# Two attention items instead of one in each place between projection passes, with the steps around them moved and four probability buffers

## The chip, the cores and the metric

The kernel runs on one core of one Trainium2 chip. The metric is the time of one execution on the device in microseconds (us); the times given are medians of runs. Engines: TensorE (PE in the profile, PEld for its weight loads), VectorE (DVE), ScalarE (ACT), GpSimd (POOL) and SyncE (SP, which here issues most DMAs).

## The reference

Two layers over x of 512 tokens by 1024 channels in float32. A layer normalizes x, projects it onto 9,292 columns and feeds three branches:

- A: 8 heads of sparse attention. An indexer scores the keys, the 128 best of each query are kept, and softmax runs over these.
- B: 8 heads of chunked attention with a learned bias by relative position.
- C: an mLSTM with 4 heads of 128 channels. Its q and k pass a causal convolution of 4 taps and a silu first.

```python
def hybrid_layer(x, ...):
    h = rms_norm(x, norm_g)
    proj = jnp.einsum('bsd,de->bse', h, w_in) + b_in
    ...
    y_a = indexer_sparse_attention(a_q, a_k, a_v, i_q, i_k, i_w)
    y_b = chunked_relpos_attention(b_q, b_k, b_v, rel_bias)
    y_c = mlstm_chunkwise(silu(conv(c_q)), silu(conv(c_k)), c_v, c_i, c_f + f_bias, c_o)
    y_c = head_layer_norm(y_c, c_norm_w)
    branches = jnp.stack([y_a * silu(a_z), y_b * silu(b_z), y_c * silu(c_z)], axis=2)
    y = jnp.einsum('bsnw,nwd->bsnd', branches, w_branch)
    merged = jnp.sum(sigmoid(gates) * y, axis=2)
    return x + jnp.einsum('bsd,de->bse', merged, w_out)
```

## The kernel before, in words

**The projection.** It is cut into 49 units of 128 columns. Weights and activations are split into a high and a low float32r part, and a unit is 24 passes, matmuls of 128x128 weights with 512 columns (`product`, L626): 16 with the high weights (`w_hi`), then 8 with the low ones (`w_lo`). ScalarE makes the high part of a unit's weights (`high_part`, L825) and GpSimd the low part (`split`, L588), in two slots by turns. Units add up in two banks, `acc`, by turns. When a unit is done, ScalarE reads it out (`read_sums`, L854) and makes the high part of the unit after next. Units 16 to 48 are bq (up to 12 before), bk, bv (17 to 20), cq and ck (21 to 28), cv (29 to 32), az, bz (33 to 40), co, cz. Behind the units come a loop that merges the branches and the output projection.

**The items.** Branch A has items 0 to 31, item n being head n % 8 of query block t = n // 8; branch B items 32 to 63 and branch C items 64 to 79, with head (n - 32) // 4 or (n - 64) // 4 and block t = n % 4. An item of block t works on (t + 1) * 128 keys, in steps:

- `scores`: TensorE makes the scores in one of two banks (L722, L728; for C L737 to L744), VectorE adds the mask or bias and takes the maximum into a buffer of `prob` (L1302), which frees the bank.
- `exp`: ScalarE's exponential in `prob` (L1014, for C L1027).
- `turn_p`: TensorE transposes it (L753) into one of two banks, ScalarE copies it out to `prob_t` (L1038). For C VectorE multiplies instead (L1312).
- `values`: TensorE multiplies it with the values (L766, L773); behind every fourth item (every second of C) VectorE divides by the sums (L1322 to L1335).

**The order.** `schedule` (L84) writes out one list of steps, and each engine runs its own part of it in that order. Steps between two `CUT`s are a group. `interleave` (L233) sets the groups of a unit at even distances between the 24 passes of the next unit, so that a group is a place where TensorE leaves the passes for small matmuls. `push(n)` (L90) makes one group: the scores of item n, the exponential of item n - 1, the transposes of n - 2 and the values of n - 3 (for C all but the scores one item later: exponential of n, transposes of n - 1, values of n - 2). Units 17 to 37 have three or four such groups each, units 38 to 41 four and one for the z unit. Behind a group's attention steps stand, in the same place of each queue: a round of `topk` on VectorE (L1266, L1267); the stacks, that is the high and low parts of q and k of a head (`bq_hi`, `bk_hi` on ScalarE, L982 to L992; `bq_lo`, `bk_lo` on VectorE, L1250 to L1261), at the items of `STACK_AT` (L75 to L81); `rel_bias`, a DMA that ScalarE issues (L1004); and the steps below.

**Steps in the middle of a unit.** `conv` (L1271) runs on VectorE, for units 21 to 28, in two parts of two taps each; `conv_gate` is a tanh on ScalarE (L995) and a product on VectorE (L1287) that waits for it. Part 0 stands behind the last group of a unit, part 1 behind the first group of the next (`soon`), the gate behind its second (`late`). `turn_v` (TensorE and ScalarE), `y_split` (ScalarE L1042, then VectorE L1350) are in `late` too. `rows` (L1353 to L1372, with an Exp and an Ln on ScalarE, L1045 and L1047) stand one per unit behind item 31 on. `z_a`, `z_b` (L777, L1337) have groups of their own in units 34 to 41: TensorE transposes the branch's output into the bank `spare`, VectorE multiplies it with the read-out unit, and ScalarE's read-out of the next such unit waits for that (L863). `turn_c` (L785, L1373) uses `spare` as well.

```python
    for u in range(first, U_BZ):
        units(u, u + 1)
        upto = -(-64 * (u + 1 - first) // (U_BZ - first))
        k = 0
        while n < upto:
            push(n)
            if work:
                seq.append(work.pop(0))
            seq.extend(STACK_AT.get(n, []))
```

Of the kernel before, what the change touches and what calls it, by code (L numbers as in the profile page):

```python
# [26 lines left out]
P = 128  # L27
DEPTH, SEQ, D = 2, 512, 1024
NT = SEQ // P
DC = D // P  # L30
HEADS, HD = 8, 64
IDX_HEADS = 4
TOPK = 128
# [45 lines left out]
for h in range(1, HEADS):  # L79
    for n, kind in ((28, "bq_hi"), (29, "bk_hi"), (29, "bq_lo"), (30, "bk_lo")):  # L80
        STACK_AT.setdefault(n + 4 * h, []).append((kind, h))  # L81


def schedule(l):  # L84
# [5 lines left out]
    def push(n):  # L90


        seq.append(CUT)
        if n is not None:
            seq.append(("scores", n))
        flying.append(n)
        mlstm = any(m is not None and m >= 64 for m in flying[-4:])
        for back, kind in ((1, "exp"), (2, "turn_p"), (3, "values")) if mlstm else ((2, "exp"), (3, "turn_p"), (4, "values")):
            if len(flying) >= back and flying[-back] is not None:
                seq.append((kind, flying[-back]))  # L100

    def flush():
        for _ in range(3):
            push(None)
        flying.clear()
# [56 lines left out]
    for u in range(first, U_BZ):  # L162

        units(u, u + 1)
        upto = -(-64 * (u + 1 - first) // (U_BZ - first))
        k = 0
        while n < upto:
            push(n)
            if work:
                seq.append(work.pop(0))  # L170
            seq.extend(STACK_AT.get(n, []))
            if n == 31:
                rows = 0
            if n >= 32 and n % NT == NT - 1 and (n - 32) // NT + 2 < HEADS:
                seq.append(("rel_bias", (n - 32) // NT + 2))
            n += 1
            if k == 0:
                seq.extend(soon)
                soon = []
            if k == 1:  # L180
                seq.extend(late)
                late = []
                if rows == 6:
                    seq.append(("row_parts", 0))
                    rows += 1
                if u == U_AZ + 1:
                    seq.append(("turn_c", 0))
            k += 1
# [15 lines left out]
    for u in range(U_BZ, U_CO):  # L204
        units(u, u + 1)
        for k in range(NT):
            push(n)
            n += 1
            if k == 2:
                seq.extend(late)  # L210
                late = []
# [114 lines left out]
def build(nc, x_in, x_tok_in, w_full, w_mix, params_in, rel_in, gains_in, consts_in, out, x_kept):  # L326
    ctx = ExitStack()
    with ctx:
# [80 lines left out]
        ones = sb("ones", [P, SEQ])  # L409
# [7 lines left out]
        prob = sb("prob", [P, 3, SEQ])  # L417
# [202 lines left out]
        def _(pe):  # L620
# [57 lines left out]
            for l in range(DEPTH):  # L678
                for kind, n in SEQUENCES[l]:
# [67 lines left out]
                    elif kind == "turn_p":  # L747
                        branch, h, t = item(n)
                        if branch != "c":
                            pe.wait_ge(turn_free[n % 2], l * (ITEMS // 2) + n // 2 + FREE)  # L750
                            pe.wait_ge(prob_ready, l * ITEMS + n + 1)
                            for s in range(t + 1):
                                last = pe.transpose(ps_t[n % 2][:, s * P:(s + 1) * P], prob[:, n % 3, s * P:(s + 1) * P], ident)  # L753
# [65 lines left out]
        def _(act):  # L819
# [24 lines left out]
            for l in range(DEPTH):  # L844
# [65 lines left out]
                for kind, n in SEQUENCES[l]:  # L910
# [99 lines left out]
                    elif kind == "exp":  # L1010
                        branch, h, t = item(n)
                        if branch != "c":
                            act.wait_ge(max_ready, l * 64 + n + 1)
                            act.activation(prob[:, n % 3, 0:(t + 1) * P], prob[:, n % 3, 0:(t + 1) * P], ACT.Exp,  # L1014
                                           bias=neg_max[:, n % 4:n % 4 + 1], scale=-1.0,
                                           accum_out=row_sum[:, n % 8:n % 8 + 1]).then_inc(prob_ready, 1)
                        else:
                            use = SCORE_USE[("scores", n)]
                            act.wait_ge(score_full, l * SCORE_USES + use + 1)
                            if n < 67:  # L1020
                                act.wait_ge(turn_full, l * ITEMS + n - 2)
                            else:
                                act.wait_ge(turn_free[(n - 3) % 2], l * (ITEMS // 2) + (n - 3) // 2 + 1 + FREE)
                            if n == 64:
                                act.wait_ge(spare_free, l * SPARE_USES + SPARE_USE[("turn_c", 0)] + 3 + FREE)
                            for s in range(t + 1):
                                last = act.activation(prob[:, n % 3, s * P:(s + 1) * P], ps_s[use % 2][:, s * P:(s + 1) * P],  # L1027
# [76 lines left out]
        def _(dve):  # L1104
# [52 lines left out]
            for l in range(DEPTH):  # L1157
# [10 lines left out]
                for kind, n in SEQUENCES[l]:  # L1168
# [120 lines left out]
                    elif kind == "scores":  # L1289
# [3 lines left out]
                        if branch != "c":  # L1293
# [8 lines left out]
                            dve.tensor_tensor_reduce(out=prob[:, n % 3, 0:w], in0=ps_s[use % 2][:, 0:w], in1=mask, scale=-1.0,  # L1302
                                                     scalar=3.0e38, op0=ALU.add, op1=ALU.min,
                                                     accum_out=neg_max[:, n % 4:n % 4 + 1]).then_inc(max_ready, 1)
                    elif kind == "turn_p":
                        branch, h, t = item(n)
                        if branch == "c":
# [4 lines left out]
                            dve.scalar_tensor_tensor(prob_t[:, n % 2, 0:w], ps_t[n % 2][:, 0:w], 0.25 * P ** -0.5, prob[:, n % 3, 0:w],  # L1312
# [47 lines left out]
                    elif kind == "rows":  # L1360
# [3 lines left out]
                        link(dve.tensor_tensor_scan(decay[:, SUM_AT[s]:SUM_AT[s] + w], ones[0:CH, 0:w], f_row[:, s * P:SEQ], 0.0,  # L1364
# [175 lines left out]
```

## Time and profile before

| what | us |
|---|---|
| median of 3 runs (1302.51 to 1303.42) | 1303.11 |
| the profiled execution's own time | 1301.93 |
| its span, from the first instruction to the last | 1300.1 |
| TensorE busy | 1268.2 |
| VectorE busy | 697.6 |
| ScalarE busy | 618.4 |
| GpSimd busy | 601.6 |

The span is what the trace covers; 1.8 us of the execution lie outside it. Matmuls overlap in their records, and a record runs on for some time after the next has started, so what a matmul costs is read from one start to the next. The first layer's items lie between 113 and 363 us of the span, the second layer's between 750 and 1000 us, in the same pattern.

### The profile page before, as it was taken

What the parts mean: (1) busy time and instruction counts of PE and PEld (TensorE: products, weight loads), DVE (VectorE), ACT (ScalarE), POOL (GpSimd) and SP (SyncE); (2) the same over time, 40 slices, a digit from 0 to 9 for tenths busy, and PEclk for the clock granted to TensorE, in tenths of its full rate; (3) what the DMA queues carried; (4) which work ended last, traced back from release to release, by engine and by line L of the source; (5) the groups of instructions that cost most, each with busy time, mean ns of one, the idle gap of its engine ahead of it and who ended that gap; (6) DMA issues with size and microseconds to landing.
All of it is one profiled execution on the core that took longest, in us unless ns stands there. A gap on an engine that the chain in (4) does not pass through costs nothing.

```text
span 1300.1 us, 19666 instructions
## 1 busy us (share of the span) xinstructions
PE 1268.2 (98%) x6462; PEld 1063.8 (82%) x6462; DVE 697.6 (54%) x1422; ACT 618.4 (48%) x1119; POOL 601.6 (46%) x759
## 2 busy tenths in 40 slices
PE   8999999999999999999999999999999999999997
PEld 6787888888987888887878888888888878888875
DVE  6789797854445221123687888886544631121143
ACT  6444667675534332333244466677654433323332
POOL 6654333422235555455675633343322455455462
PEclk9999999999999999999999999999999999999998
DMA  7223111221322323323242221112112222332331
GB/s 276 97 83 110 68 50 57 69 86 49 112 68 61 108 82 97 107 87 120 87 160 83 96 87 60 50 65 90 58 49 103 85 81 83 103 99 86 105 97 65
DMA packets 37047, 116.35 MB, mean 89 GB/s; under 512 B 4080, under 2 KB 4464, under 8 KB 36720
## 3 DMA queue, kind: packets, MB, share of 16 engines
q1 hardware_dynamic: 34672, 111.24, 25.8%
q10 hardware_dynamic: 2304, 4.20, 1.1%
q8 instruction: 41, 0.67, 0.2%
q14 instruction: 30, 0.25, 0.1%
HBM read 111.23 MB, written 4.19 MB: 89 GB/s over the span
## 4 chain that ended last, share of the span: by engine, by line
PE 82%; DVE 10%; ACT 4%; issue 3%; POOL 1%; DMA 0%; ACTq 0%; SPq 0%; DVEq 0%; POOLq 0%
PE acc L639 66%; PE ps_o L766 4%; PE ps_t L753 3%; DVE score L1267 2%; PE ps_t L744 2%; PE ps_o L773 1%; PE ps_s L722 1%; DVE top L1266 1%; PE ps_s L728 1%; DVE att_c L1399 1%; DVE ak_s L1240 1%; PE spare L704 1%; ACT prob L1014 1%; PE ps_s L737 1%; PE spare L783 1%
## 5 line engine op out<-in xcount | busy, mean ns | idle before, releaser
L593 POOL TENSOR_TENSOR w_lo<-w_raw,w_hi 128x256 fp32r<-128x256 f32 x744 | 588.6, 820 | 674.9 <-ACT w_hi L831 674.6
L639 PE MATMUL acc<-h_hi,w_hi 128*128 128x512 f32 x1120 | 448.1, 400 | 1.6 <-POOL h_lo L604 1.6
L639 PE MATMUL acc<-h_lo,w_hi 128*128 128x512 f32 x1120 | 439.2, 392 | 0.0
L639 PE MATMUL acc<-h_hi,w_lo 128*128 128x512 f32 x1120 | 293.0, 395 | 1.3 <-POOL w_lo L593 1.3
L831 ACT ACTIVATE w_hi<-w_raw 128x1024 fp32r<-128x1024 f32 (+1 forms) x210 | 201.9, 961 | 120.8 <-PE acc L639 92.0
L639 PEld LDWEIGHTS acc<-h_hi,w_hi 128*128 128x128 f32 x1120 | 210.8, 188 | 41.9 <-POOL h_lo L604 2.5
L639 PEld LDWEIGHTS acc<-h_lo,w_hi 128*128 128x128 f32 x1120 | 210.8, 188 | 39.0
L639 PEld LDWEIGHTS acc<-h_hi,w_lo 128*128 128x128 f32 x1120 | 205.3, 188 | 41.5 <-POOL w_lo L593 1.8
L1412 DVE SCALAR_TENSOR_TENSOR gated<-prob,acc 128x512 f32<-128x512 f32 x16 | 11.0, 687 | 247.6 <-PE acc L639 247.6
L1064 ACT ACTIVATE prob<-acc,par_half 128x512 f32<-128x512 f32 x48 | 33.1, 690 | 148.1 <-PE acc L639 148.1
L1014 ACT ACTIVATE prob<-prob,neg_max 128x128 f32<-128x128 f32 (+3 forms) x128 | 70.6, 552 | 19.7 <-DVE neg_max L1302 19.2
L1038 ACT ACTIVATE prob_t<-ps_t 128x128 f32<-128x128 f32 (+3 forms) x128 | 54.3, 425 | 34.2 <-PE ps_t L753 34.2
L753 PE MATMUL ps_t<-consts,prob 128*128 128x128 f32 x320 | 56.6, 275 | 7.1 <-ACT prob L1014 6.8
L1266 DVE MAX8 top<-score 128x8 f32<-128x256 f32 (+2 forms) x96 | 53.6, 558 | 1.6
L1302 DVE CUSTOM_DVE_ANT_0 prob<-ps_s,rel 128x128 f32<-128x128 f32 (+1 forms) x64 | 31.2, 490 | 40.6 <-PE ps_s L728 39.8
L1267 DVE MATCH_REPLACE8 score<-top,score 128x256 f32<-128x256 f32 (+2 forms) x96 | 52.1, 543 | 0.0
L639 PE MATMUL acc<-merged_hi,w_hi 128*128 128x512 f32 x128 | 50.8, 397 | 1.1 <-DVE merged_lo L1421 1.1
L753 PEld LDWEIGHTS ps_t<-consts,prob 128*128 128x128 f32 x320 | 38.9, 140 | 15.3 <-issue 10.4
L639 PE MATMUL acc<-merged_lo,w_hi 128*128 128x512 f32 x128 | 50.6, 395 | 0.0
L1412 DVE SCALAR_TENSOR_TENSOR z<-prob,acc 128x512 f32<-128x512 f32 x32 | 22.0, 687 | 50.8 <-PE acc L639 50.8
L1281 DVE SCALAR_TENSOR_TENSOR turn<-pad,par,turn 128x512 f32<-128x512 f32 x48 | 46.1, 961 | 1.5
L766 PE MATMUL ps_o<-av,prob_t 128*128 128x64 f32 x320 | 43.0, 265 | 1.3 <-issue 1.3
(242 smaller groups left out, 1787.9 us busy)
## 6 DMA issues: line engine op xcount, KB each, us to landing
w_raw<-w_full SPq DMA_DIRECT2D x162, 512.0 KB, 3.4
w_raw<-w_mix SPq DMA_DIRECT2D x48, 256.0 KB, 2.6
rel<-rel ACTq DMA_DIRECT2D x16, 256.0 KB, 2.6
xT<-x SPq DMA_DIRECT2D x4, 512.0 KB, 6.4
stage<-x_tok SPq DMA_DIRECT2D x4, 512.0 KB, 10.2
xT<-x SPq DMA_DIRECT2D x1, 2048.0 KB, 10.8
x_kept<-xT SPq DMA_DIRECT2D x1, 2048.0 KB, 9.0
xT<-x_kept SPq DMA_DIRECT2D x1, 2048.0 KB, 8.3
```

What stands on the lines that cost most here:

```text
L593: last = pool.tensor_tensor(w_lo[:, slot, part, :], w_raw[:, raw, part, :], w_hi[:, slot, part, :].bitcast(F32), ALU.subtract)
L639: last = pe.matmul(acc[slot][:, :], w[:, slot, k, :], x[:, k, :], start=(i == 0), stop=(i == 3 * nk - 1))
L753: last = pe.transpose(ps_t[n % 2][:, s * P:(s + 1) * P], prob[:, n % 3, s * P:(s + 1) * P], ident)
L766: last = pe.matmul(ps_o[:, place * HD:(place + 1) * HD], prob_t[:, n % 2, s * P:(s + 1) * P], v[:, s, f:f + HD], start=(s == 0), stop=(s = ...
L831: act.activation(w_hi[:, slot, 0:nk, :], w_raw[:, raw, 0:nk, :], ACT.Copy).then_inc(w_hi_done, 1)
L1014: act.activation(prob[:, n % 3, 0:(t + 1) * P], prob[:, n % 3, 0:(t + 1) * P], ACT.Exp, bias=neg_max[:, n % 4:n % 4 + 1], scale=-1.0, accu ...
L1038: act.activation(prob_t[:, n % 2, 0:(t + 1) * P], ps_t[n % 2][:, 0:(t + 1) * P], ACT.Copy)\
L1064: act.activation(prob[:, b, :], acc[slot_of(l, PROJ + b)][:, :], ACT.Tanh, bias=par_half[:, bass.ds(i * 2 + (C_GATE + DC * b + j), 1)], sc ...
L1266: link(dve.max(top8[:, :], s))
L1267: link(dve.match_replace(s, top8[:, :], s, TAKEN))
L1281: ins = dve.scalar_tensor_tensor(turn[:, :], x[:, tap:tap + SEQ], w, turn[:, :], ALU.mult, ALU.add)
L1412: dve.scalar_tensor_tensor((gated, z, z)[b][:, :], prob[:, b, :], 1.0, acc[slot_of(l, PROJ + 3 + b)][:, :], ALU.add, ALU.mult)\
```

## The change

- An attention place holds two items, n and n + 1: both scores, both exponentials, the transposes of the two before, the values of the two before these. With items of C in flight the transposes (VectorE's product) are those of the same two items, and the values those of the two before. `push(None)` of the three flushes becomes one or two empty places.
- The items of a unit, 3 or 4 before, are 2 or 4, so that units have one or two such places.
- All steps of `soon` and `late` stand behind the first place of a unit: part 1 of a convolution and its gate in one place.
- Stacks of B: `bq_hi` and `bk_hi` of head h behind item 27 + 4h, `bq_lo` and `bk_lo` behind item 29 + 4h.
- `prob` has four buffers instead of three; the array `ones` has 128 columns instead of 512, and the scan of `rows` reads one column of it as a broadcast.

```diff
+PROBS = 4
...
-    for n, kind in ((28, "bq_hi"), (29, "bk_hi"), (29, "bq_lo"), (30, "bk_lo")):
+    for n, kind in ((27, "bq_hi"), (27, "bk_hi"), (29, "bq_lo"), (29, "bk_lo")):
         STACK_AT.setdefault(n + 4 * h, []).append((kind, h))
...
-    def push(n):
+    def push(*items):
         seq.append(CUT)
-        if n is not None:
-            seq.append(("scores", n))
-        flying.append(n)
-        mlstm = any(m is not None and m >= 64 for m in flying[-4:])
-        for back, kind in ((1, "exp"), (2, "turn_p"), (3, "values")) if mlstm else ((2, "exp"), (3, "turn_p"), (4, "values")):
-            if len(flying) >= back and flying[-back] is not None:
-                seq.append((kind, flying[-back]))
+        seq.extend(("scores", n) for n in items)
+        flying.append(items)
+        seq.extend(("exp", n) for n in items)
+        lag = 0 if any(n >= 64 for new in flying[-2:] for n in new) else 1
+        for back, kind in ((lag, "turn_p"), (lag + 1, "values")):
+            if len(flying) > back:
+                seq.extend((kind, n) for n in flying[-1 - back])

     def flush():
-        for _ in range(3):
-            push(None)
+        push()
+        if not any(n >= 64 for new in flying for n in new):
+            push()
         flying.clear()
...
-        upto = -(-64 * (u + 1 - first) // (U_BZ - first))
+        upto = 2 * -(-32 * (u + 1 - first) // (U_BZ - first))
         k = 0
         while n < upto:
-            push(n)
-            if work:
-                seq.append(work.pop(0))
-            seq.extend(STACK_AT.get(n, []))
-            if n == 31:
-                rows = 0
-            if n >= 32 and n % NT == NT - 1 and (n - 32) // NT + 2 < HEADS:
-                seq.append(("rel_bias", (n - 32) // NT + 2))
+            push(n, n + 1)
+            for n in (n, n + 1):
+                if work:
+                    seq.append(work.pop(0))
+                seq.extend(STACK_AT.get(n, []))
+                if n == 31:
+                    rows = 0
+                if n >= 32 and n % NT == NT - 1 and (n - 32) // NT + 2 < HEADS:
+                    seq.append(("rel_bias", (n - 32) // NT + 2))
             n += 1
             if k == 0:
-                seq.extend(soon)
-                soon = []
-            if k == 1:
-                seq.extend(late)
-                late = []
+                seq.extend(soon + late)
+                soon, late = [], []
...
-        for k in range(NT):
-            push(n)
-            n += 1
+        for k in range(0, NT, 2):
+            push(n, n + 1)
+            n += 2
...
-        ones = sb("ones", [P, SEQ])
+        ones = sb("ones", [P, P])
...
-        prob = sb("prob", [P, 3, SEQ])
+        prob = sb("prob", [P, PROBS, SEQ])
...
-                            if n < 67:
-                                act.wait_ge(turn_full, l * ITEMS + n - 2)
+                            if n < 64 + PROBS:
+                                act.wait_ge(turn_full, l * ITEMS + n - PROBS + 1)
                             else:
-                                act.wait_ge(turn_free[(n - 3) % 2], l * (ITEMS // 2) + (n - 3) // 2 + 1 + FREE)
+                                act.wait_ge(turn_free[(n - PROBS) % 2], l * (ITEMS // 2) + (n - PROBS) // 2 + 1 + FREE)
...
-                        link(dve.tensor_tensor_scan(decay[:, SUM_AT[s]:SUM_AT[s] + w], ones[0:CH, 0:w], f_row[:, s * P:SEQ], 0.0,
+                        link(dve.tensor_tensor_scan(decay[:, SUM_AT[s]:SUM_AT[s] + w], ones[0:CH, 0:1].broadcast_to([CH, w]), f_row[:, s * P:SEQ], 0.0,
```

## Rows read from the trace of the kernel before

**Rows 1.** The page, part 1: busy time, share of the span, instructions.

```profile
PE 1268.2 (98%) x6462; PEld 1063.8 (82%) x6462; DVE 697.6 (54%) x1422; ACT 618.4 (48%) x1119; POOL 601.6 (46%) x759
```

**Rows 2.** Chain that ended last: start us, us, what.

```profile
406.62 196.60 PE acc L639 x864
```

**Rows 3.** Timeline of TensorE, two places: start us, us, instruction.

```profile
371.14 0.60 PE L798 MATMUL spare<-consts,z_tanh 128*128 128x128 f32 x4
...
371.81 0.40 PE L639 MATMUL acc<-h_lo,w_hi 128*128 128x512 f32 x1
...
204.99 0.61 PE L722 MATMUL ps_s<-ak_s,aq_s 128*128 128x512 f32 x2
205.45 0.60 PE L753 MATMUL ps_t<-consts,prob 128*128 128x128 f32 x4
205.88 1.00 PE L766 MATMUL ps_o<-av,prob_t 128*128 128x64 f32 x8
...
207.01 0.39 PE L639 MATMUL acc<-h_lo,w_hi 128*128 128x512 f32 x1
```

**Rows 4.** Windows: PE, PEld, DVE, ACT, POOL busy (count), clock, DMA share, GB/s.

```profile
116.00:130.00 14.00, 12.79 (x67) 10.55 (x66) 13.33 (x43) 7.95 (x24) 5.78 (x7) 1.00 0.22 70
170.00:222.00 52.00, 49.70 (x295) 42.92 (x295) 43.06 (x85) 35.82 (x70) 18.61 (x20) 1.00 0.14 46
222.00:280.00 58.00, 57.74 (x350) 50.49 (x349) 40.61 (x89) 42.93 (x94) 23.31 (x25) 1.00 0.26 87
280.00:314.00 34.00, 32.58 (x202) 27.80 (x201) 18.53 (x40) 20.59 (x46) 9.31 (x12) 1.00 0.18 55
314.00:363.00 49.00, 48.84 (x336) 43.77 (x336) 22.92 (x61) 23.47 (x56) 11.18 (x16) 1.00 0.26 86
```

**Rows 5.** Timeline of ScalarE and then TensorE around 213 to 221 us.

```profile
213.88 0.63 ACT L1045 ACTIVATE norm<-norm 4x512 f32<-4x512 f32 x1
214.53 1.28 ACT L1047 ACT_TABLE_LOAD   x1
...
218.37 1.28 ACT L1014 ACT_TABLE_LOAD   x1
...
218.37 0.39 PE L728 MATMUL ps_s<-bk_lo_s,bq_s 128*128 128x512 f32 x1
220.41 0.41 PE L753 MATMUL ps_t<-consts,prob 128*128 128x128 f32 x2 [1.65 <-ACT prob L1014]
```

**Rows 6.** VectorE's waits, 154 to 250 us: us in total, times, longest.

```profile
DVE prob L1302 <- PE ps_s L722: 6.1, 6, 1.9
DVE ck L1287 <- ACT z_tanh L995: 3.2, 2, 2.1
DVE prob L1302 <- PE ps_s L728: 2.7, 3, 1.3
```

**Rows 7.** Groups of VectorE, 116 to 363 us: busy us, mean ns | idle before.

```profile
L1281 DVE SCALAR_TENSOR_TENSOR turn<-pad,par,turn 128x512 f32<-128x512 f32 x24 | 23.1, 961 | 0.7
...
L1266 DVE MAX8 top<-score 128x8 f32<-128x512 f32 x16 | 11.0, 688 | 0.0
L1267 DVE MATCH_REPLACE8 score<-top,score 128x512 f32<-128x512 f32 x16 | 10.8, 675 | 0.0
...
L1302 DVE CUSTOM_DVE_ANT_0 prob<-ps_s,rel 128x512 f32<-128x512 f32 x8 | 5.5, 690 | 1.2 <-PE ps_s L728 1.1
...
L1278 DVE TENSOR_SCALAR turn<-pad,par 128x512 f32<-128x512 f32 x8 | 4.3, 544 | 0.2
...
L1287 DVE SCALAR_TENSOR_TENSOR ck<-z_tanh,turn 128x512 f32<-128x512 f32 x4 | 2.8, 692 | 3.2 <-ACT z_tanh L995 3.2
```

**Rows 8.** The same groups of ScalarE.

```profile
L831 ACT ACTIVATE w_hi<-w_raw 128x1024 fp32r<-128x1024 f32 x24 | 25.4, 1060 | 4.7 <-ACT pad L906 2.8 <-ACT z L867 2.0
...
L1014 ACT ACTIVATE prob<-prob,neg_max 128x512 f32<-128x512 f32 x16 | 11.4, 712 | 3.8 <-DVE neg_max L1302 3.8
...
L995 ACT ACTIVATE z_tanh<-turn 128x512 f32<-128x512 f32 x8 | 5.1, 633 | 7.3 <-DVE turn L1281 6.3 <-DVE neg_max L1302 0.9
```

More of the change, by code:

```diff
@@ L752, in _ @@
                             for s in range(t + 1):
-                                last = pe.transpose(ps_t[n % 2][:, s * P:(s + 1) * P], prob[:, n % 3, s * P:(s + 1) * P], ident)
+                                last = pe.transpose(ps_t[n % 2][:, s * P:(s + 1) * P], prob[:, n % PROBS, s * P:(s + 1) * P], ident)
                             last.then_inc(turn_full, 1)
@@ L1013, in _ @@
                             act.wait_ge(max_ready, l * 64 + n + 1)
-                            act.activation(prob[:, n % 3, 0:(t + 1) * P], prob[:, n % 3, 0:(t + 1) * P], ACT.Exp,
+                            act.activation(prob[:, n % PROBS, 0:(t + 1) * P], prob[:, n % PROBS, 0:(t + 1) * P], ACT.Exp,
                                            bias=neg_max[:, n % 4:n % 4 + 1], scale=-1.0,
@@ L1026, in _ @@
                             for s in range(t + 1):
-                                last = act.activation(prob[:, n % 3, s * P:(s + 1) * P], ps_s[use % 2][:, s * P:(s + 1) * P],
+                                last = act.activation(prob[:, n % PROBS, s * P:(s + 1) * P], ps_s[use % 2][:, s * P:(s + 1) * P],
                                                       ACT.Exp, bias=source_t[:, s, h:h + 1])
@@ L1300, in _ @@
                                 mask = key_mask[:, MASK_AT[t]:MASK_AT[t] + w] if t else consts[:, K_CHUNK:K_CHUNK + P]
-                            dve.tensor_tensor_reduce(out=prob[:, n % 3, 0:w], in0=ps_s[use % 2][:, 0:w], in1=mask, scale=-1.0,
+                            dve.tensor_tensor_reduce(out=prob[:, n % PROBS, 0:w], in0=ps_s[use % 2][:, 0:w], in1=mask, scale=-1.0,
                                                      scalar=3.0e38, op0=ALU.add, op1=ALU.min,
@@ L1311, in _ @@
                             w = (t + 1) * P
-                            dve.scalar_tensor_tensor(prob_t[:, n % 2, 0:w], ps_t[n % 2][:, 0:w], 0.25 * P ** -0.5, prob[:, n % 3, 0:w],
+                            dve.scalar_tensor_tensor(prob_t[:, n % 2, 0:w], ps_t[n % 2][:, 0:w], 0.25 * P ** -0.5, prob[:, n % PROBS, 0:w],
                                                      ALU.mult, ALU.mult).then_inc(turn_free[n % 2], 1)
```

## The prediction

> **What bounds the kernel now.** I read the page first. TensorE is busy for 98% of the span [rows 1], and its granted clock is 1.00 in every stage shown [rows 4], so the question is what stands between its matmuls. The chain of waits answers it for the back of a layer: 864 passes in 196.60 us, 0.2275 us each, with nothing between them [rows 2]. The change leaves that part alone. It touches units 16 to 41 of each layer, about 113 to 363 us and 750 to 1000 us, where attention's small matmuls stand in "places" between the passes of the projection.
>
> What does a place cost? The timeline of TensorE shows one place with 4 small matmuls and one with 2 wide and 12 small [rows 3]. The first takes 371.81 - 371.14 = 0.67 us up to the second pass behind it; less that one pass, 0.44, or 0.111 each. The second takes 207.01 - 204.99 - 0.227 = 1.79; less two 512-column matmuls (0.455), 1.34 for 12, again 0.111 each. A place thus has a price per matmul and none of its own.
>
> So only waits can be won or lost. By stage [rows 4] TensorE idles 2.30 us in 170 to 222, 0.26 in 222 to 280, 1.42 in 280 to 314 and 0.16 in 314 to 363. Records run over the start of a wait: the wait in [rows 5] is 1.65 in its row, but 220.41 - 218.37 less a pass is 1.8. With 0.15 more for each of some ten waits these stages hold about 3.5, 2.1 and 0.3 us (170 to 280, 280 to 314, 314 to 363); 1.6 more lie at the first items (116 to 130: 1.21 idle and three such overlaps) [rows 4]. That is 7.5 us a layer, 15 us in all: the most that the change can win.
>
> VectorE is the engine behind it: busy 43.06 of 52 us and 40.61 of 58 [rows 4]. Between 154 and 250 us it waits 8.8 us for scores and 3.2 for the tanh of the convolution [rows 6].
>
> **The change, part by part.**
>
> Places: 85 attention places a layer become 43, with the same matmuls. By [rows 3] this saves 42 x 0 = 0 on TensorE. The fit of those two places leaves about 0.03 us a place open either way, so the bounds are -1.3 and +1.3 us a layer; I take 0, the value both rows give.
>
> Four probability buffers, the smaller array of ones, its broadcast in the scan: the same count of instructions on VectorE; a shorter fill on GpSimd, hidden behind the load of x at the start. 0; without that cover it would be some tenths of a us, once.
>
> Stacks of branch B, and the bias DMAs on ScalarE's queue: same instructions and DMAs, at other items. Their users stand two places later as before. 0 by themselves; they count below as work in the queues.
>
> Convolution (units 21 to 28, eight a layer). Here I see the cost. Before, part 1 of a convolution stands in one place and its gate in the next, so ScalarE's tanh runs while VectorE does something else; only two of the eight gates wait, 3.2 us [rows 6]. After, both sets of steps go behind the same first place: VectorE finishes part 1 and stands at the gate until ScalarE has run the tanh (0.63, [rows 8]) and both handoffs (0.15): at least 0.8 x 8 = 6.4 us. Queued behind the waiting gate are the next part 0 and the next two masks; for those wait ScalarE's exponentials, and TensorE for both. ScalarE itself runs the tanh only after two exponentials, two copies and the stack copies of that place.
>
> How much of it reaches TensorE? I laid the three queues beside each other from the scores of items 16 and 17 (0 us, the trace's 155), with [rows 7] and [rows 8]: a topk round 0.69 + 0.68 and a short load between, 1.46, a mask of 512 columns 0.69, part 0 of a convolution 0.54 + 0.96 = 1.5, part 1 1.94, gate 0.7, an exponential 0.71, the high part of a unit 1.06. Waits of TensorE that come out:
> - at 22.9 (scores 24, 25): VectorE comes from gate 0 and part 0 of the next at 22.4, so masks 22, 23 end at 22.9 and 23.4; the copies of items 20, 21 stand behind those exponentials and free the transposes' banks at 24.7 and 25.2. Wait 1.1.
> - at 31.4 (scores 26, 27): the same with gate 1, done at 30.8. Wait 1.25.
> - ScalarE then is late: masks 30, 31 at 50.6, their exponentials and two copies to 52.6, stacks to 54.5, Exp, table load and Ln to 57.15, unit 26 read out and unit 28's high part to 59.0 (TensorE wants it at 59.65), table load, exponentials 32, 33 and copies to 62.35, tanh to 62.95. VectorE has stood at gate 4 since 58.85. It runs gate, rows and part 0 until 67.2 before masks 34, 35, and TensorE is there at 66.3: wait 2.1.
> - the debt stays: masks 40, 41 wait for part 0 of the last convolution until 89.1, TensorE is there at 85.8: wait 3.7.
> - small ones at 45.7, 96.8 and 101.6: 0.8.
>
> Sum 9.0 a layer, against about 3.5 in the same stretch now: **+5.5**. Bounds: +8.9 (all of the eight gates' added idle, 12.1 by this laying less the 3.2 of now, in TensorE's way) and -3.5 (all present waits gone and no new one). I take +5.5, as laid: VectorE has little reserve there, 8.8 us of waits for scores [rows 6], and what lies of it ahead of the convolutions can't take up what the gates add.
>
> The wait of now behind the table load goes: load, exponential, transpose in line [rows 5]. After, 20 passes (4.5 us) stand between the scores of items 32, 33 and their transposes. Late next is the gate named above; this is in the 9.0.
>
> A load takes 1.28 us and starts 0.02 us after the Exp before it [rows 5]. The Trainium skill, "ScalarE: Activation LUTs", What ACT_TABLE_LOAD costs, adds a drain of about 1.38 us to every switch; the trace shows none. By that page ScalarE would reach unit 28's high part 0.7 us too late for TensorE, and the sum would be some 1.5 us higher over both layers.
>
> Units 34 to 37: the transposes there wait because ScalarE reads out the z unit late, behind VectorE's gated product (1.42 idle, [rows 4]). With pairs there is a whole place and 6 passes or more behind the exponentials; only one wait, of z_a1 for the spare bank behind turn_c, comes out (0.4). 2.1 becomes 0.5: **-1.6**. Bounds -2.1 and 0.
>
> mLSTM items: values one place after their scores, 6 passes (1.36 us) and the next pair's scores between; the read-out of a unit holds ScalarE about 2.5 us. By the same laying it fits with 0.1 to spare in units 38 to 40 and misses by 0.5 in unit 41, where 4 and 5 passes stand; the present 0.3 at the last item goes. **+0.2**; bounds -0.3 and +2. First items: the masks still wait for the same topk rounds, 0.
>
> Sum a layer: 0 + 5.5 - 1.6 + 0.2 = +4.1; a hand laying tends to add up small lags that real slack takes away, and I take 3.7. Two layers: +7.4. Against the profiled execution (1301.93 us, span 1300.1) that is 1309.3; the median of the runs is 1.2 higher (1303.11), so **1310.5**.
>
> **The rivals.**
> A. Pairs give slack and nothing is given back (faster). For it: the wait behind the table load (1.8) and the z stage (1.7) and the last mLSTM item (0.3) each have their mechanism removed; if ScalarE is free at each gate, a gate costs 0.8 and VectorE's waits for scores take that up. It decides at whether the masks of items 34 to 41 are done when TensorE comes for the banks: if VectorE's debt stays below about 3 us there, nothing is lost. Then -3.8 a layer: 1303.1 - 7.6 = 1295.5. Against it: VectorE busy 43 of 52 us.
> B. Waits change places only: the new ones equal the lost 3.8 a layer. 1303.
> C. The debt also reaches the read-out: where a unit has one place, ScalarE reads out a finished unit only behind the tanh, and the high part of the unit after next comes late. My laying leaves 0.65 us at unit 28; 1 us less at each of four such units and TensorE stops at their start: +4 a layer more, 1318.
> D. The place has a price of its own that two rows don't show; bounds above, inside A and B.
>
> **How the numbers follow.** Forecast case (1306 to 1315) 0.44, C (to 1320) 0.08, B (1300.5 to 1305.7) 0.16, A (1290 to 1300.4) 0.32. About 0.2%, 2.6 us, is what a measurement of this kernel can tell. Slower 0.52, same 0.16, faster 0.32. The range leaves out half of A's lower side and what exceeds C: 1295 to 1319; the forecast's own range is 1306 to 1315.
>
> **What would show it.** Right: VectorE's wait for z_tanh rises from 3.2 to about 12 us a layer, TensorE's idle in the second half of the convolutions' stretch from 0.26 to 4 or more, all behind VectorE's masks; the transposes' wait behind the table load and in units 34 to 37 is gone. A pass stays 0.227. Wrong: if the gates wait near 0.8 each and the masks of items 34 to 41 are never waited for, A holds; if the time falls though the waits stay, places did have a price.

## The result, and the profile after

| | before | after |
|---|---|---|
| median of 4 runs each (us) | 1302.88 | 1316.59 |
| lowest to highest | 1302.51 to 1303.42 | 1314.73 to 1317.74 |
| ratio, with its 95% interval | | 1.0105 [1.0093, 1.0118] |
| the profiled execution | 1301.93 | 1317.74 |
| its span | 1300.1 | 1316.0 |

The change costs 13.7 us. It is slower, as forecast. The time lies inside the stated 1295 to 1319, but 1.6 us above the forecast case's own 1306 to 1315; the forecast was +7.4.

The page's part 1 and its clock line (40 slices, the granted clock in tenths), of after:

```profile
PE 1279.5 (97%) x6462; PEld 1073.1 (82%) x6462; DVE 699.0 (53%) x1422; ACT 613.9 (47%) x1119; POOL 595.7 (45%) x759
PEclk9999999999999999999999999988999999999998
```

Counts are those of [rows 1]: no instruction was added. New are the two slices at 8 ahead of the end, some 855 to 920 us; the 8 in the last slice stands in before too. The chain of waits gives the loss by layer; its rows of 864 passes start 7.76 us later than [rows 2] in the first layer, and in the second, where the chain of before has its row at 1044.04, 15.86 later. Of the first 7.76 us, 1.6 are lost near 35 us, ahead of all that was changed, in a spell at half clock (last section). So the items of the first layer lose 6.2 us and those of the second 8.1:

```profile
414.38 196.59 PE acc L639 x864
...
1059.90 196.60 PE acc L639 x864
```

Windows of after, columns as in [rows 4], where the last two rows cut out the place of the loss:

```profile
116.00:130.00 14.00, 13.34 (x72) 11.02 (x71) 13.37 (x43) 8.12 (x22) 6.04 (x8) 1.00 0.17 59
170.00:222.00 52.00, 50.91 (x299) 43.36 (x297) 41.16 (x81) 34.39 (x67) 15.76 (x19) 1.00 0.15 52
222.00:280.00 58.00, 53.39 (x294) 45.97 (x295) 39.22 (x85) 39.38 (x88) 18.88 (x23) 0.94 0.23 77
280.00:314.00 34.00, 32.35 (x204) 28.29 (x203) 21.06 (x44) 21.23 (x48) 10.86 (x12) 1.00 0.18 56
314.00:363.00 49.00, 49.00 (x338) 44.16 (x338) 20.91 (x56) 24.79 (x60) 13.45 (x20) 1.00 0.26 87
222.00:262.00 40.00, 35.39 (x184) 30.07 (x185) 32.95 (x66) 24.73 (x57) 13.28 (x15) 0.91 0.18 60
864.00:904.00 40.00, 36.36 (x175) 30.48 (x174) 31.15 (x63) 23.71 (x55) 13.56 (x16) 0.83 0.19 60
```

TensorE idles 4.61 us in 222 to 280, where it was 0.26, and here its mean clock is 0.94. Elsewhere little is left or gained: it idles 1.09 in 170 to 222 for 2.30 before, 0 for 0.16 in 314 to 363, and 1.65 for 1.42 in 280 to 314. Waits of VectorE (154 to 256 us, the same masks as 154 to 250 in before), then of TensorE (116 to 370 us): us in total, times, longest.

```profile
DVE ck L1287 <- ACT z_tanh L995: 8.4, 4, 4.1
DVE cq L1287 <- ACT z_tanh L995: 2.8, 4, 0.7
DVE prob L1302 <- PE ps_s L728: 2.6, 2, 1.4
DVE prob L1302 <- PE ps_s L722: 2.2, 2, 1.9
```

```profile
PE ps_s L728 <- DVE neg_max L1302: 4.1, 3, 2.5
PE spare L783 <- DVEq L1377: 1.6, 1, 1.6
PE ps_t L753 <- ACT prob_t L1038: 1.6, 3, 0.6
PE ps_s L722 <- DVE neg_max L1302: 0.6, 1, 0.6
```

All eight gates now wait for the tanh, 11.2 us against 3.2 [rows 6], and the waits of VectorE for scores fell from 8.8 to 4.8: of its reserve about half is used up. TensorE's waits for exponentials ([rows 5] shows the longest) are gone; in before this was their line:

```profile
PE ps_t L753 <- ACT prob L1014: 3.3, 5, 1.7
```

In their place TensorE waits 4.7 us for VectorE's masks, which it did once and for 1.0 us in before, and 1.6 each for `spare` and for ScalarE's copies of transposes.

The longest gate wait and the mask behind it, timeline of VectorE, then ScalarE in the same us, then TensorE:

```profile
212.51 1.54 DVE L1281 SCALAR_TENSOR_TENSOR turn<-pad,par,turn 128x512 f32<-128x512 f32 x2
218.16 0.69 DVE L1287 SCALAR_TENSOR_TENSOR ck<-z_tanh,turn 128x512 f32<-128x512 f32 x1 [4.11 <-ACT z_tanh L995]
218.89 0.68 DVE L1358 SCALAR_TENSOR_TENSOR f_row<-f_row,norm 4x512 f32<-4x512 f32 x1
219.60 1.21 DVE L1359 TENSOR_TENSOR_SCAN run_max<-f_row,i_iw_row 4x512 f32<-4x512 f32 x1
220.85 0.79 DVE L1278 TENSOR_SCALAR turn<-pad,par 128x512 f32<-128x512 f32 x1
221.68 1.10 DVE L1281 SCALAR_TENSOR_TENSOR turn<-pad,par,turn 128x512 f32<-128x512 f32 x1
222.82 0.56 DVE L1302 CUSTOM_DVE_ANT_0 prob<-ps_s,rel 128x384 f32<-128x384 f32 x1
```

```profile
213.28 1.06 ACT L831 ACTIVATE w_hi<-w_raw 128x1024 fp32r<-128x1024 f32 x1 [0.17 <-ACT pad L906]
214.36 1.28 ACT L1014 ACT_TABLE_LOAD   x1
215.66 0.40 ACT L1014 ACTIVATE prob<-prob,neg_max 128x128 f32<-128x128 f32 x1
...
216.55 1.06 ACT L1038 ACTIVATE prob_t<-ps_t 128x512 f32<-128x512 f32 x2
217.50 0.63 ACT L995 ACTIVATE z_tanh<-turn 128x512 f32<-128x512 f32 x1
```

```profile
221.57 0.39 PE L639 MATMUL acc<-h_lo,w_hi 128*128 128x512 f32 x1
223.44 0.33 PE L728 MATMUL ps_s<-bk_hi_s,bq_s 128*128 128x128 f32 x1 [1.48 <-DVE neg_max L1302]
```

VectorE has ended part 1 at 214.05 and stands until 218.16. ScalarE is at that time behind its own list: weights, a table load, the exponentials and copies of the place, and only then the tanh. Behind the gate stand the rows and part 0 of the next convolution, so the masks of items 34 and 35 start at 222.82, and TensorE, ready at 221.80 (221.57 and a pass), starts at 223.44: 1.64 us. This is gate 4, and the wait is that of the forecast's third station. ("Station" is used here for each of the four large waits of TensorE in the forecast's list: 22.9, 31.4, 66.3 and 85.8 us behind 155, so 177.9, 186.4, 221.3 and 240.8.)

**How each stretch is read.** Here and below "excess" is the time from each start on TensorE to the next, less 0.228 per 512 columns (0.173 for 384) and at least 0.111 per small matmul, near the prices of [rows 2] and [rows 3]; it is what waits and slow passes cost, free of overlaps in records. A price of 0.227 would add 0.3 to each entry of the long stretch, in all kernels alike. Of each kernel one profiled execution, first layer / second layer:

| excess, us | before | after | gate behind part 1 in before (b_gate_next) | gate a place later (a_gate_later) | unread matmuls in waits (a_fill_all) |
|---|---|---|---|---|---|
| 116–130 / 753–768 | 1.66 / 1.60 | 1.41 / 1.21 | 1.65 / 1.67 | 1.39 / 0.34 | 1.37 / 1.24 |
| 170–280 / 808–917 | 3.6 / 3.7 | 10.9 / 13.2 | 9.5 / 8.5 | 0.6 / 0.4 | 4.2 / 4.2, and 5.9 of them |
| 280–314 / 917–951 | 2.15 / 2.43 | 1.71 / 1.71 | 2.59 / 2.19 | 1.81 / 1.97 | 1.84 / 1.79 |
| 314–363 / 951–1000 | 0.24 / 0.22 | -0.22 / -0.18 | -0.21 / 0.47 | -0.27 / -0.19 | -0.32 / -0.24 |

The last column's 5.9 us are 26 unread matmuls of 0.227 a layer.

### The profile page after: what moved, and what is told of

Its sections match the earlier page's. It is cut to its first block, busy times and chain, and to the rows that moved or that the text cites. A ratio compares the mean times of both kernels' runs of the same rounds, so it can differ in the third digit from the quotient of the medians.

```text
span 1316.0 us, 19638 instructions
## 1 busy us (share of the span) xinstructions
PE 1279.5 (97%) x6462; PEld 1073.1 (82%) x6462; DVE 699.0 (53%) x1422; ACT 613.9 (47%) x1119; POOL 595.7 (45%) x759
## 4 chain that ended last, share of the span: by engine, by line
PE 74%; DVE 17%; ACT 5%; issue 2%; POOL 1%; DMA 0%; ACTq 0%; SPq 0%; DVEq 0%; POOLq 0%
PE acc L639 61%; PE ps_o L766 3%; DVE score L1267 2%; DVE top L1266 2%; DVE turn L1281 2%; PE ps_t L753 2%; PE ps_t L744 1%; PE ps_o L773 1%; DVE prob L1302 1%; PE ps_s L728 1%; DVE att_c L1399 1%; DVE bk_lo_s L1259 1%; PE ps_s L722 1%; DVE turn L1278 1%; ACT prob L1014 1%
## 5 line engine op out<-in xcount | busy, mean ns | idle before, releaser
L639 PEld LDWEIGHTS acc<-h_hi,w_lo 128*128 128x128 f32 x1120 | 211.3, 192 | 45.2 <-POOL w_lo L593 1.8
L753 PE MATMUL ps_t<-consts,prob 128*128 128x128 f32 x320 | 48.1, 280 | 3.8 <-ACT prob_t L1038 3.6
L1038 ACT ACTIVATE prob_t<-ps_t 128x128 f32<-128x128 f32 (+3 forms) x128 | 48.1, 419 | 6.1 <-PE ps_o L766 6.1
L766 PE MATMUL ps_o<-bv,prob_t 128*128 128x64 f32 x320 | 42.3, 283 | 0.0
L766 PEld LDWEIGHTS ps_o<-bv,prob_t 128*128 128x128 f32 x320 | 41.5, 205 | 0.2
```

The costliest lines, as they stand in the source:

```text
L639: last = pe.matmul(acc[slot][:, :], w[:, slot, k, :], x[:, k, :], start=(i == 0), stop=(i == 3 * nk - 1))
L766: last = pe.matmul(ps_o[:, place * HD:(place + 1) * HD], prob_t[:, n % 2, s * P:(s + 1) * P], v[:, s, f:f + HD], start=(s == 0), stop=(s = ...
L1038: act.activation(prob_t[:, n % 2, 0:(t + 1) * P], ps_t[n % 2][:, 0:(t + 1) * P], ACT.Copy)\
```

## The experiments

Twelve kernels; each ratio is to the kernel before on the same chip, with its 95% interval. Names beginning with b_ are edits of the kernel before, with a_ of the one after; "pairs" are the two items in one place. The expectations put two theories against each other: by theory 1 the loss is the gate's wait for the tanh, by theory 2 it is the coarser order of the pairs.

**b_gate_next: only the gate moves, in the kernel before.** One item per place and everything else stays.

```diff
-            late.append(("conv_gate", u - U_CQ))
+            soon.append(("conv_gate", u - U_CQ))
```

> The kernel before, with one item per place as it is, and only the gate of a convolution moved up behind part 1, in the first place of a unit. If the gate behind part 1 is what costs (theory 1), VectorE's waits for z_tanh rise from 3.2 us a layer to 6 or more and part of that reaches TensorE: 2 to 8 us slower than before. If the loss needs the pairs, because two masks and two exponentials stand behind each other and the banks are wanted one place earlier (theory 2), this kernel stays within 2 us of the kernel before, though its gates wait.

Measured 1315.13 us against 1302.19, 1.0100 [1.0083, 1.0117], +12.9: this one word gives nearly the whole loss. The waits of VectorE, and those of TensorE (same stretches as above):

```profile
DVE ck L1287 <- ACT z_tanh L995: 2.8, 4, 0.7
DVE cq L1287 <- ACT z_tanh L995: 2.8, 4, 0.7
```

```profile
PE ps_t L753 <- ACT prob L1014: 6.0, 8, 1.7
PE ps_o L766 <- issue: 1.3, 1, 1.3
```

Every gate waits exactly 0.7, the round trip for the tanh. VectorE waits for the tanh only 2.4 us longer than before, and yet TensorE loses 5 to 6 us a layer. The gate and its wait, 1.4 us, now stand ahead of the next mask, and the delay comes out at the transposes: TensorE's waits there for exponentials are 6.0 us in eight places, for 3.3 in five. That it comes out there because with one item per place the transposes follow their scores soon is argued, not shown. So the place of the gate is dear in both kernels, but by another wait than in the kernel after. The loss is above the 2 to 8 us of theory 1 and the 2 of theory 2; a spell at half clock (last section) is part of it.

**a_no_tanh and b_no_tanh: the wait taken away in both.** The tanh of the silu is left out and the gate reads `turn` alone.

```diff
-                        act.wait_ge(conv_sum, l * 8 + n + 1)
-                        act.activation(z_tanh[:, :], turn[:, :], ACT.Tanh, scale=0.5).then_inc(conv_tanh, 1)
+                        continue
...
-                        dve.wait_ge(conv_tanh, l * 8 + n + 1)
+                        dve.wait_ge(conv_sum, l * 8 + n + 1)
...
-                        dve.scalar_tensor_tensor(dst, z_tanh[:, :], 1.0, turn[:, :], ALU.add, ALU.mult).then_inc(conv_done, 1)
+                        dve.scalar_tensor_tensor(dst, turn[:, :], 1.0, turn[:, :], ALU.add, ALU.mult).then_inc(conv_done, 1)
```

> The changed kernel without the tanh of the convolution's gate, so nothing of ScalarE's is waited for at the gate; VectorE's two instructions stay. It leaves the tanh out of silu. Theory 1: the gates' wait (11.2 us a layer) was the loss, so the waits of TensorE for masks at 221 and 243 us go and the time falls by 9 us or more, to 1307 or below, with the granted clock at 1.00 in the items. Theory 2: VectorE's debt comes from the coarser order, and the time falls by less than 4 us.

> The kernel before, with the same tanh left out: the control. Its gates wait 3.2 us a layer now and ScalarE gets 5 us of work less; both theories expect 0 to 3 us less than before, 1300 to 1303.

Measured: after 1295.52, 0.9944 [0.9928, 0.9961]; before 1301.75, 0.9995 [0.9986, 1.0005]. Leaving the tanh out is worth nothing that shows in before (0.4 us) and 21 us in after, as theory 1 had it. Without it the kernel with pairs is 6.2 us faster than the one without. In a_no_tanh TensorE is busy nearly without a gap in the stretch that idled 4.61:

```profile
170.00:222.00 52.00, 51.85 (x315) 45.30 (x314) 46.79 (x89) 34.77 (x71) 19.01 (x20) 1.00 0.19 61
222.00:280.00 58.00, 57.29 (x341) 49.63 (x340) 40.34 (x90) 41.99 (x94) 20.15 (x24) 1.00 0.25 79
```

**a_conv_first: other work between part 1 and the gate, in the same place.** Part 1 and the tanh go right behind the attention steps; topk rounds and stacks stand between them and VectorE's gate.

```diff
             push(n, n + 1)
+            if k == 0:
+                seq.extend(soon)
+                seq.extend(("conv_tanh", step[1]) for step in late if step[0] == "conv_gate")
+                soon = []
```

> The changed kernel with the same steps, pairs kept: in the first place of a unit, part 1 of the convolution and ScalarE's tanh stand right behind the attention steps, and the topk rounds and stacks stand between them and VectorE's gate. Theory 1: the gates' wait falls from 11.2 us a layer to under 3 and the time by 6 us or more. Theory 2: less than 3 us.

Measured 1302.18, 0.9999 [0.9990, 1.0009]: the time of before, 14.4 us under after. The time is as theory 1 had it; the gates' wait, expected under 3 us, is 4.6. Four waits of 0.7 (cq) are gone and 4.6 of 8.4 (ck) is left, the longest 3.2, at gate 4 as in after.

**a_gate_later: the gate one place later, the tanh left behind part 1.** The sums of two convolutions are then alive at once, so they alternate between `turn` and `gated`.

```diff
             push(n, n + 1)
+            seq.extend(gates)
+            gates = []
...
-                seq.extend(soon + late)
+                seq.extend(soon)
+                gates = [step for step in late if step[0] == "conv_gate"]
+                seq.extend(("conv_tanh", step[1]) for step in gates)
+                seq.extend(step for step in late if step[0] != "conv_gate")
...
+                        total = (turn, gated)[n % 2]
```

> The changed kernel with whole computation: ScalarE's tanh right behind part 1 of a convolution, VectorE's gate one place later (even and odd convolutions sum up in two buffers, so that the next may start). Pairs kept. If the gates' waits were the only loss and the pairs themselves win what the two kernels without a tanh show (6.2 us), the gates wait near 0 and the time is 1295 to 1298, faster than before. If ScalarE's queue stays the bound, the gates still wait over 3 us a layer and the time is 1301 or more.

Measured 1293.61 against 1301.79, 0.9936 [0.9922, 0.9949]. No gate waits, and its windows show idle time of 0.15 us at most and no drop of the clock:

```profile
170.00:222.00 52.00, 52.00 (x316) 45.82 (x316) 47.63 (x94) 38.64 (x78) 20.24 (x21) 1.00 0.20 63
222.00:280.00 58.00, 57.85 (x345) 50.53 (x344) 41.59 (x87) 42.96 (x96) 21.06 (x24) 1.00 0.26 81
```

That is faster than the 1295 to 1298 expected. No instruction is left out against the kernel after, so the whole step from +13.7 to -8.2 is one of place. The 7.3 us of excess in the stretches of the convolutions of before (3.6 + 3.7) are down to 1.0: this is what the pairs are good for. That it is not only the wait at the gates shows in b_no_tanh, where these waits are gone too and the same stretches still have 3.5 and 3.4.

**a_gate_turnc: that, and turn_c right behind the attention steps.** It is aimed at z_a1's wait for `spare`.

```diff
+            if k == 0 and u == U_AZ + 1:
+                seq.append(("turn_c", 0))
...
-                if u == U_AZ + 1:
-                    seq.append(("turn_c", 0))
```

> The same, with turn_c right behind the attention steps of its place instead of behind the stacks and y_split, so that z_a1 finds the spare bank free. If TensorE's wait of 1.8 us at L783 around 290 us is VectorE's two copies standing behind those steps, it goes: 3 to 3.6 us less than a_gate_later over two layers. If it is passed on to the next wait (VectorE's gated product, ScalarE's read-out of the z unit), less than 1 us.

Measured 1291.36 against 1301.79, 0.9920 [0.9907, 0.9934]: 10.4 us under before, the best of all. The wait of 1.8 for `spare` is gone, but a part of it comes back in another place, timeline of TensorE:

```profile
292.64 0.28 PE L733 MATMUL ps_s<-bk_lo_s,bq_s 128*128 128x256 f32 x1
293.65 0.55 PE L758 MATMUL ps_t<-consts,prob 128*128 128x128 f32 x3 [0.73 <-ACT prob_t L1043]
```

The excess of 280 to 314 goes from 1.81 to 0.87, and 1.97 to 1.00 in the second layer: 1.9, for 2.25 measured. The gain lies between the two outcomes that the expectation names.

**b_ones_prob: four buffers, the small array of ones and its broadcast, in the kernel before.**

```diff
-        ones = sb("ones", [P, SEQ])
+        ones = sb("ones", [P, P])
...
-        prob = sb("prob", [P, 3, SEQ])
+        prob = sb("prob", [P, PROBS, SEQ])
...
```

> The kernel before with four probability buffers, the array of ones at 128 columns and the broadcast in the scan, nothing else. All theories expect no change: 1302 to 1304. Only if the earlier start of TensorE's first matmuls (ones are filled 0.4 us sooner) changes its clock at the head, 1.5 us more.

Measured 1302.09 against 1301.79, 1.0002 [0.9993, 1.0012]: nothing, as the forecast had it.

**a_stacks_old and a_later_stacks_old: the stacks at their old items**, in the kernel after and in a_gate_later.

```diff
-    for n, kind in ((27, "bq_hi"), (27, "bk_hi"), (29, "bq_lo"), (29, "bk_lo")):
+    for n, kind in ((28, "bq_hi"), (29, "bk_hi"), (29, "bq_lo"), (30, "bk_lo")):
```

> The changed kernel with branch B's stacks at the items of before (28, 29, 29, 30). Theory 1 (the gates): the stack copies stand on ScalarE ahead of the tanh in either case, at other gates; within 2 us of the changed kernel, 1314 to 1318. If the stacks' new items were what delayed ScalarE (its tanh 4.1 us late at the longest wait), 4 us or more faster.

> a_gate_later (gates one place later, pairs kept) with branch B's stacks at the items of before. With the gates right behind part 1 those items cost 7.7 us more. If that came through the gates and VectorE's debt, here it costs under 1.5 us: 1293 to 1295. If the low parts of k come too late for the first scores of a head in any case (the pair's first place is one place behind them), 4 us or more: 1298 or above.

Measured 1324.29, 1.0169 [1.0154, 1.0185], which is 7.7 over after; and 1310.76 against 1302.04, 1.0068 [1.0055, 1.0082], some 17 us above a_gate_later. The first of these was a clear miss of mine (1314 to 1318 expected); the second is as expected if the low parts come too late. Waits of VectorE and TensorE in a_later_stacks_old:

```profile
DVE bq_s L1258 <- ACT bq_s L992: 9.7, 4, 4.9
```

```profile
PE ps_s L733 <- DVE bk_lo_s L1264: 5.6, 3, 3.3
```

In pairs items 28 and 29 (32 and 33 for the first of these heads) share a place, so VectorE's `bq_lo` stands in the place of ScalarE's `bq_hi` and waits for it: the same fault as the gate's, at another step. `bk_lo` then comes in the last place ahead of the scores of its head. With 27 and 29 the high parts stand a place ahead, and neither wait is there. The moved stacks are not neutral: they are what the pairs need.

**a_rows_later: rows from item 33 on instead of 31**, to take their Exp, Ln and table loads out of ScalarE's way at gate 4.

> The changed kernel with the steps rows (Exp and Ln on ScalarE with their table load) one unit later, behind item 33 instead of 31. If gate 4's wait of 4.1 us comes from ScalarE's table loads standing ahead of its tanh, it falls to about 0.8 at this gate but one of the next two gates pays part of it; the time falls by 2 to 8 us. If it stands only behind masks and exponentials, it stays and the time is within 1 us of the changed kernel.

Measured 1317.13, 1.0117 [1.0100, 1.0133]: no gain. The waits of ck are 8.5 in total for 8.4, but they have moved. Timeline of VectorE, gates 4 and 5:

```profile
215.07 1.15 DVE L1287 SCALAR_TENSOR_TENSOR ck<-z_tanh,turn 128x512 f32<-128x512 f32 x1 [0.70 <-ACT z_tanh L995]
...
226.96 0.69 DVE L1287 SCALAR_TENSOR_TENSOR ck<-z_tanh,turn 128x512 f32<-128x512 f32 x1 [5.18 <-ACT z_tanh L995]
```

Gate 4 waits 0.70 for 4.11 in after, and gate 5, ahead of which Exp, Ln and the two table loads now stand, 5.18 for 1.66. So ScalarE's lag at gate 4 does come from these steps, and a place one unit later only hands it to the next gate; this half of the expectation came true, the gain of 2 to 8 us did not.

**a_fill and a_fill_all: is it the clock?** The granted clock fell in the kernel after (below). Unread matmuls of 512 columns into `spare` stand ahead of the scores of items 36 and 42, where TensorE would wait: 6 and 8 in a_fill, 7 and 19 in a_fill_all, whose edit this is.

```diff
+                        for _ in range({36: 7, 42: 19}.get(n, 0)):
+                            pe.matmul(spare[:, :], h_hi[:, 0, 0:P], h_hi[:, 0, :], start=True, stop=True)
```

> The changed kernel with 6 matmuls of 512 columns that nobody reads (1.36 us) just before the scores of item 36 and 8 (1.8 us) before those of item 42, in the two places where TensorE waits 1.6 and 2.7 us for a bank anyway. If its waits there are what is followed by spells at half the granted clock, these go, the clock is 1.00 from 220 to 260 and from 860 to 905 us, and the time falls by the 8 us that passes and small matmuls lose in them, to 1308 to 1310; if the spells have another cause, they stay and the time does not fall.

> The changed kernel with 7 and 19 unread matmuls (1.6 and 4.3 us) before the scores of items 36 and 42, since with 6 and 8 TensorE still waited 2.7 us at item 42 and one spell at half clock stayed. If a wait of TensorE is what goes ahead of a spell, none is left from 220 to 260 and 860 to 905 us. Then what the spells cost can be read: if they add to the waits, 1309 to 1312 (they hold 20 us at half clock); if VectorE sets the time of these places and the spells only fill its waits, within 2 us of the changed kernel.

a_fill: 1317.61 against 1301.85, 1.0119 [1.0102, 1.0135], no gain, where 1308 to 1310 was expected. The spells at 226 and 868 were gone; TensorE came earlier to item 42, still waited (2.3 for the mask), and the spell behind it at 247 was twice as long. a_fill_all: 1312.19 against 1302.04, 1.0076 [1.0063, 1.0090], with no spell left in either layer's items:

```profile
222.00:262.00 40.00, 38.85 (x220) 33.03 (x220) 32.20 (x67) 26.02 (x60) 12.94 (x16) 1.00 0.21 71
864.00:904.00 40.00, 38.84 (x217) 32.71 (x217) 32.53 (x68) 25.71 (x58) 12.96 (x16) 1.00 0.21 68
```

VectorE's waits for the tanh are as in after, 8.4 and 2.8. It is 10.15 us slower than before (1312.19 less 1302.04), where after is 13.7 slower, each against the kernel before measured beside it; that leaves 3.6 us for the clock, and the two medians taken as they stand 4.4 (1316.59 less 1312.19). So 3.6 to 4.4 of the 13.7 us go with the clock, and some 9.3 to 10.1 are the waits. Unread matmuls that outlast the waits they fill would raise the clock's share; this was not measured.

## Why the prediction was right or wrong

**The number.** The sign and the mechanism came true. The size did not: +13.7 for +7.4, and 1316.59 lies where the forecast had put the outcomes of rival C (up to 1320, chance 0.08) and not its own. That it is inside the range is owed to the room left for C, whose mechanism is not what happened; this part is luck. Of the 6.3 us missed, 2.7 are waits whose sum was too small (10.15 less 7.4, with a_fill_all for full clock), and the rest, 3.6, goes with the clock.

**Places 0: borne out, within the bounds.** With half of the places, a_gate_later has an excess of 0.6 and 0.4 in the convolutions' stretches, priced by matmuls alone; a place that cost much more than [rows 3] say would have made it negative. The -0.2 to -0.3 in 314 to 363 leave room for some tenths a layer. The bounds of 1.3 stand (rival D).

**Buffers, array of ones, broadcast 0: right**, by b_ones_prob.

**The gates: right in mechanism and nearly in size.** Forecast 12.1 us of gate waits a layer, measured 11.2 (+8.0 on before instead of +8.9). The four stations came in the order and within 3 us of the places laid by hand, 6.7 us in sum for 8.2:

| forecast at (us of trace) | wait forecast | measured at | measured |
|---|---|---|---|
| 177.9 | 1.1 | 179.8 | 0.67 |
| 186.4 | 1.25 | 188.0 | 0.71 |
| 221.3 | 2.1 | 221.6 | 1.64, 0.34, 0.68 in one place |
| 240.8 | 3.7 | 243.5 | 2.65 |

"What lies of it ahead of the convolutions can't take up what the gates add" held: VectorE's waits for scores fell by 4.0 us, not enough for 8.0. The step +5.5 a layer compares with 10.9 - 3.6 = 7.3 and 13.2 - 3.7 = 9.5, clock included. At full clock (a_fill_all) it is 4.2 + 5.9 - 3.6 = +6.5. Not all of that must be waits: the unread matmuls may be a few tenths longer than the waits they fill. The fourth station is larger at full clock than in the table: 2.65 us stand in the trace of after only since TensorE came to it late from a spell of 3.4 us; in a_fill_all 19 unread matmuls, 4.3 us, stand there for the 3.7 forecast.

**The clock: not in the forecast at all.** "A pass stays 0.227" is wrong behind four of TensorE's waits (last section). This is the largest miss, 3.6 to 4.4 of the 6.3 us between +7.4 and +13.7.

**Units 34 to 37: mis-sized.** The step was forecast at -1.6, from 2.1 to 0.5; the excess went from 2.15 to 1.71 and from 2.43 to 1.71, so -0.4 and -0.7. The number that failed is z_a1's wait for `spare` behind turn_c, named at 0.4. Timeline of TensorE, and of ScalarE:

```profile
296.64 0.39 PE L639 MATMUL acc<-h_lo,w_hi 128*128 128x512 f32 x1
298.68 0.66 PE L783 MATMUL spare<-consts,att_a 128*128 128x128 f32 x4 [1.65 <-DVEq L1377]
```

```profile
301.73 0.69 ACT L866 ACTIVATE z_tanh<-acc,par_half 128x512 f32<-128x512 f32 x1 [6.11 <-DVE gated L1345]
```

298.68 - 296.64 less a pass is 1.8. VectorE frees `spare` only behind the low stacks and y's low part of that place, and the forecast gave this 0.4 in all. ScalarE's wait of 6.11 holds no one up: behind 298.68 TensorE has no wait for 17 us.

**mLSTM items and first items: better than forecast.** 0.24 to -0.22 and 0.22 to -0.18, so -0.4 instead of +0.2; the miss by 0.5 at unit 41 did not come. The first items gave 0.25 and 0.4 where 0 was taken, though in that stretch of the second layer a_gate_later has 0.34, so its size differs between executions or kernels by more than that.

**The cut from 4.1 to 3.7** ("small lags that real slack takes away") took the wrong side: at full clock the sum is near 5.1 a layer (10.15 / 2) for 4.1 laid.

**Stacks "0 by themselves": the sum is right, the reason wrong.** It compared with their users, two places later as before. It did not ask where the high part that `bq_lo` waits for is made. Had the change left the stacks at their old items, the same argument would have given the same 0, and the time would have been 7.7 us longer.

**Rivals.** A, pairs win, has the right mechanism and was refused by the gates: take their wait away and 1293.6 to 1295.5 comes out, for 1295.5 forecast. Its deciding point, a debt of VectorE below about 3 us at items 34 to 41, was missed. C, the debt reaching the read-out at four units, would give a time near the measured one, 1318, by another cause: its waits, TensorE at the start of a unit for high parts, are not in the list of waits, and the excess is at masks. B is excluded by the interval of the ratio.

**The table load's drain.** In the rows above the weights' high part ends at 214.34, the load starts at 214.36, and the exponential follows 0.02 us behind its end. The Trainium skill, "ScalarE: Activation LUTs", What ACT_TABLE_LOAD costs, adds a drain of about 1.38 us to a switch. The trace of after disagrees, as that of before did: there is no such time on either side of the load, and nothing of the miss can be put down to it.

## What to carry to other kernels

A step that takes another engine's answer wants that engine's whole backlog of the place as work between itself and the request, and not just the answer's 0.6 us; when work is grouped more coarsely, go through every pair of producer and consumer (here gates and stacks) and ask whether both have now fallen into one place. What half as many places win, 6 to 8 us here, is lost twice over by one step that was one place apart before. A long step on the answering engine, such as two table loads, was not got rid of here by moving it: it went to the next request (a_rows_later). And a wait of the bounding engine can cost more than its length, as here behind four of them, where the clock was lower.

## What the runs showed of the hardware that was not expected

TensorE's clock fell behind waits. Windows of 4 us of after, columns as in [rows 4]:

```profile
224.00:228.00 4.00, 3.44 (x18) 3.05 (x19) 2.28 (x5) 3.58 (x10) 0.06 (x1) 0.76 0.55 193
...
248.00:252.00 4.00, 4.00 (x23) 3.56 (x22) 3.19 (x5) 0.84 (x2) 0.00 (x0) 0.76 0.27 110
868.00:872.00 4.00, 3.65 (x15) 3.50 (x16) 2.28 (x6) 2.87 (x9) 0.00 (x0) 0.50 0.63 201
892.00:896.00 4.00, 4.00 (x17) 3.71 (x18) 3.23 (x8) 1.21 (x3) 0.00 (x0) 0.50 0.11 43
```

A granted clock of 0.50 is the lower of its two levels, 1.2 of 2.4 GHz. The spells are about 3.4 us long in the first layer and 6.8 in the second, each after TensorE had stood for 1.2 to 2.7 us, and a pass in one takes nearly twice its 0.227: 0.445 on average in this row of TensorE's timeline (8 passes, 3.56 us to the next start):

```profile
871.04 3.72 PE L639 MATMUL acc<-h_hi,w_lo 128*128 128x512 f32 x8
874.60 0.40 PE L639 MATMUL acc<-h_hi,w_hi 128*128 128x512 f32 x1
```

The excess of the starts inside the spells adds up to 3.2 us in the first layer and 6.2 in the second, but taking the spells away wins 3.6 to 4.4 and not 9.4: a TensorE that is sooner back waits longer for VectorE at the next station (2.65 us in after, 4.3 us of unread matmuls in a_fill_all). Two things stay open. Not every wait has a spell behind it: in b_gate_next one of 1.8 us at 223 has none and one of the same length at 170.5 has; the 1.8 of before [rows 5] has none either. And a spell of 3.4 us near 34 us stands in the profiled executions of five of the fourteen kernels, after's among them and before's not, where the change touches nothing; it is worth 1.6 us of an execution, and is part of the 15.8 us between the two profiled executions.
